# Order of TensorE's work within a chunk: expert sums ahead of the next half's mixer slices

## The reference

```python
x = x + y @ w_out                    # y: pooling, window attention, short convolution, differential attention
x = x + peer_ffn(rms_norm(x, norm2_g), w_query, sub_keys, peer_u, peer_v)
...
h = jnp.einsum('thkd,td->thk', peer_u[ib], xb)       # 8 heads x 16 experts of each token, out of 16384
a = (gb * jax.nn.gelu(h, approximate=False)).astype(xb.dtype)
out = jnp.einsum('thk,thkd->td', a, peer_v[ib])
```

## Time and profile before

| | |
|---|---|
| median of 3 runs | 2962.0 us (2955.64 to 2963.01) |
| the profiled execution's own time | 2951.57 us |
| its span | 2949.8 us |
| PE busy | 2097.7 us, 71% |
| DVE busy | 2065.5 us, 70% |
| ACT busy | 1041.2 us, 35% |
| gathers | 1024, 1073.81 MB, 87.8% of 16 DMA engines' span |
| mean granted clock of TensorE | 0.842 |

### The profile page before, as it was taken

One profiled execution on the slowest core, in us unless ns is written; L12 is line 12 of the kernel. 1 busy time (PEld: TensorE's weight loads), 2 busy tenths in 40 slices (PEclk: granted clock), 3 DMA queues, 4 the chain that ended last, 5 costly groups with the idle time before them and its releaser, 6 DMA issues.

```text
span 2949.8 us, 37238 instructions
## 1 busy us (share of the span) xinstructions
PE 2097.7 (71%) x12696; PEld 1036.4 (35%) x12696; DVE 2065.5 (70%) x5215; ACT 1041.2 (35%) x3347; POOL 1194.0 (40%) x1028
## 2 busy tenths in 40 slices
PE   8888787777777876586775877667776665656565
PEld 7554454344443432243342533234343111111111
DVE  2466678977567687867567678976766766777665
ACT  2322345633233455423223345632223222222222
POOL 0034334443344334444343434543444444444443
PEclk9988999888888987888887988889898678677768
DMA  6189999999999999999999999999999999999998
GB/s 233 36 345 418 419 419 419 395 420 419 419 419 419 420 414 414 417 384 420 420 420 420 416 386 420 421 386 419 420 420 421 421 421 421 418 418 420 419 415 341
DMA packets 174350, 1173.26 MB, mean 398 GB/s; under 512 B 19280, under 2 KB 19408, under 8 KB 43088
## 3 DMA queue, kind: packets, MB, share of 16 engines
q0 software_dynamic: 147456, 1073.81, 87.8%
q1 hardware_dynamic: 26704, 97.07, 8.4%
HBM read 1168.71 MB, written 2.10 MB: 397 GB/s over the span
## 4 chain that ended last, share of the span: by engine, by line
DMA 48%; PE 22%; DVE 18%; ACT 5%; issue 5%; POOL 1%; SPq 0%; DVEq 0%; POOLq 0%; ACTq 0%
DMA gather<-experts,idx 48%; PE ysum L686 12%; DVE gather L1259 9%; PE bank L466 6%; ACT amp L915 2%; POOL gather L421 1%; ACT diag L923 1%; PE ysum L474 1%; PE bank L661 1%; ACT gel L908 1%; DVE x L1235 1%; PE bank L515 1%; DVE shared L1045 0%; DVE scratch L1206 0%; DVE scratch L1210 0%
## 5 line engine op out<-in xcount | busy, mean ns | idle before, releaser
L421 POOL DMA_INDIRECT gather<-experts,idx x1024 | 1193.8, 1166 | 1733.8 <-PE ysum L686 1411.5
L686 PE MATMUL ysum<-gather,diag 64*64 64x512 f32 x8192 | 1263.2, 769 | 728.3 <-ACT diag L923 696.7
L1259 DVE CUSTOM_DVE_ANT_0 gather<-gather,xc 128x1024 f32<-128x1024 f32 x1024 | 1229.8, 1224 | 682.8 <-DMA gather<-experts,idx 680.0
L686 PEld LDWEIGHTS ysum<-gather,diag 64*64 64x64 f32 x8192 | 365.7, 172 | 1526.9 <-ACT diag L923 906.8
L908 ACT ACTIVATE gel<-hdot 128x4 f32<-128x4 f32 x255 | 52.4, 205 | 1679.4 <-DVE hdot L1259 1679.4
L466 PE MATMUL bank<-xnT,w 128*128 128x256 f32 (+1 forms) x2048 | 467.1, 384 | 5.9 <-DVE xnT L975 5.9
L466 PEld LDWEIGHTS bank<-xnT,w 128*128 128x128 f32 x2048 | 380.0, 194 | 100.6 <-issue 42.8
L923 ACT ACTIVATE diag<-cc,amp 128x64 f32<-128x64 f32 x1020 | 267.9, 333 | 0.0
L915 ACT ACTIVATE amp<-gel,gate 128x1 f32<-128x1 f32 x1020 | 216.8, 283 | 8.3
L908 ACT ACT_TABLE_LOAD x105 | 134.7, 1283 | 1.8
L661 PEld LDWEIGHTS bank<-w,yT 128*128 128x128 f32 x768 | 87.3, 192 | 17.8 <-issue 17.8
(11 more groups left out here) (126 smaller groups left out, 1490.2 us busy)
## 6 DMA issues: line engine op xcount, KB each, us to landing
w<-weights SPq DMA_DIRECT2D x164, 512.0 KB, 7.9
gather<-experts,idx POOLq DMA_INDIRECT x1024, 15.1
gather<-weights SPq DMA_DIRECT2D x4, 1024.0 KB, 5.6
y_out<-x SPq DMA_DIRECT2D x4, 512.0 KB, 7.8
x<-x_in SPq DMA_DIRECT2D x2, 512.0 KB, 5.3
g2b<-g_rows SPq DMA_DIRECT2D x2, 512.0 KB, 11.7
x<-x_in SPq DMA_DIRECT2D x1, 1024.0 KB, 12.4
cc<-consts_in SPq DMA_DIRECT2D x1, 920.5 KB, 6.4
```

Of the source, the lines that this page charges most:

```text
L421: pool.indirect_dma_start(gather[:, n % SLOTS, :], None, uv_d[m // 2], bass.IndirectOffsetOnAxis(ap=idx[:, g % 2, k:k + 1], axis=0)).then_ ...
L686: mm = nc.tensor.matmul(ysum[outs, q * 512:(q + 1) * 512], diag[toks, n % NDIAG, :], gather[toks, n % SLOTS, DM + hf * 512:DM + (hf + 1) * ...
L1259: e = V.tensor_tensor_reduce(out=gather[:, n % SLOTS, 0:DM], in0=gather[:, n % SLOTS, 0:DM], in1=xc[:, :], scale=1.0, scalar=0.0, op0=ALU. ...
```

## The change

PE's call of `interleave` loses its argument, and so takes the order that ACT and DVE have: first Y(c), then S(c).

```diff
             for m in range(NBLK):
-                interleave(m, lambda n: mixer_pe(pe, n), peer_pe(pe, m), first, slices_first=True)
+                interleave(m, lambda n: mixer_pe(pe, n), peer_pe(pe, m), first)
```

## The result

The changed kernel takes 3364.91 us in the median of three runs (3355.66 to 3365.22), against 2962.0 us before: ratio 1.1358, 95% interval 1.1343 to 1.1373, 403 us slower. The forecast was 3360.

What follows compares the result with a forecast made beforehand. The prediction took DMA to set the pace everywhere, 10.0 to 12.5 us a chunk. Its terms 35 + 86 + 63 + 120 + 100 + 24 - 30 = 398 us gave 3350, or 3360 as median, range 3210 to 3510.

Steps and rivals of the forecast that it cites:

- Y(c): PE's expert sums of chunk c, which wait for ACT's diagonals; forecast at 6.0 us, ends 3.7 and 6.7.
- S(c): PE's slice of chunk c; forecast 1.0 or 1.4 us in attention, 3.84 in output blocks, 5.1 with a projection.
- Y of 6.0 us: PE's expert sums in each chained chunk, behind 7 us or more of idle time, take 6.0 us, not 6.67.
- cushion: Ten gather slots let DMA work on through a delay: about 10 us forgiven once in each section, -30 us.
- Attention: Chunks where DVE's biases wait for PE's scores: +86, +35 and +63 us in sections 1, 2 and 3.
- Output blocks: Chunks where DVE's addition waits for PE's block: turn 16.6 us against DMA's 11.25, +120 us over three sections.
- Plain projections: Chunks where ACT, not DVE, closes the chain: one block costs nothing, two take 14.1 against 12.5, 15 times: +24 us.
- Transitions: Chunks with transposes, last value block, first biases and norms of y: together +100 us.
- ACT's path in sections 1 and 3: Eight attention slices with a projection: ACT's copy, table loads and exponential make the longer chain, 16.5 us a turn.
- No change: Rival: DMA hides the new order, with DVE's gather waits and ten slots as slack; 2962 us, chance 0.03.
- Faster: Rival: gather slots come free earlier and the DMA dips fill, 25 us less, 2937 us; chance 0.02.
- Y at 3.7: Rival, slower by half: PE's clock stays up, expert sums take 3.7 to 4.6 us, time 3150 to 3235; chance 0.10.

Runs made afterwards that it cites:

- the last run: Kernel before, with PE's expert sums first only in the three chunks with the norms of y: 2951.45 us, ratio 0.9989 to the kernel before.
- narrow sums: Changed kernel, all four products of every second gather run over 128 of 512 columns: 3232.52 us, ratio 1.0937 to the kernel before.
- wide ones: Changed kernel, the four products of every fourth gather issued twice: 3446.74 us, ratio 1.1667 to the kernel before.

## Why the prediction was right, step by step

*DMA sets the pace before, 10.0 to 12.5 us a chunk.* Right as far as it was tried: with the sums longer by a quarter the kernel before stayed where it was. No run changed the gathers themselves.

*The chain closes where DVE's slice needs PE's of the same chunk.* Right, and shown from both sides: taking ACT's and DVE's slices a chunk later takes the whole loss away, DVE's alone 271 us of it, and the order matters little in chunks without the link (+19 us).

*Turns.* Output block: forecast 16.6, 16.8 in the turn shown and 16.3 as the mean of the seven turns of section 2 (113.8 us from its first L1166 to its last). In the turn shown Y took 6.61 us and not 6.0, with which the parts of the forecast give 17.2, so the closeness of 16.6 and 16.8 is in part luck. Attention of section 3: forecast 16.1, 17.0 in the turn shown (Y 6.45 us in it), an item over all 512 keys, where biases and scores are longer than the 384-column rows that I used.

*Y of 6.0 us.* 5.86. Choosing the level of the rows with gaps above 4 us over the 6.67 of a single one was right. By the stricter reading of the clock rule in the Trainium skill (TensorE: Matmul & The Clock Gate, "What's actually happening") the sum would have been 60 us higher; the 88 rows of Y behind gaps above 4 us, 5.86 us in the mean, speak against that size.

*Sizes of the parts.* A part that is changed alone has the forecast's whole cushion of 30 to itself. Attention: forecast 184, so 154 with the cushion off, and +194 when changed alone: too small. Output blocks: 120, so 90, and +100 alone. Plain projections: 24, so nothing, and +19 alone; the turn of two blocks was also added up wrongly (its rows give 14.3 and not 14.1, some 4 us in all). Transitions: 100, so 70, and +41 alone: too large. There the forecast counted every chunk at full excess and took nothing off for the wait that the sums escape at the norms of y, which is worth 3 to 4 us by the last run. Why the remainder was too large is open. Within the changed kernel the stretches from the first bias to the last grew by 169 us, against the 184. By section the forecast has 166, 101 and 131 when its terms and 10 us of cushion each are sorted (plain ones 18, 3 and 3; transitions 35, 30 and 35, a split made after the result); measured 173, 94 and 142. The errors of the terms cancel to some 10 us, and that is luck: the total agrees better than its terms. The cushion itself was measured by no run.

*ACT's path in sections 1 and 3.* The direction is supported by the run with DVE a chunk later (section 2 and all output blocks back, the attention of sections 1 and 3 not); its share is not settled, as said above.

*What would show it.* DMA at 6 to 8 and some 300 GB/s in the stretches: 292 GB/s in the window of section 3. In section 2 the slices with attention kept a 9, at 355 to 368 GB/s. Waits at L1045 and L1166: 468 us in place of 29. DVE's waits for gathers were to fall to some 300 and fell to 507: those of the last section (177 us before) and of the plain projections stayed, and I had not set them aside.

*Rivals.* No change needed DVE's slice not to wait; it waits. Faster: the fixed part of the turn (4.7 + 1.5 + Y) is above DMA's 10 us. Y at 3.7 did not come: PE's gaps in the turns shown are 6 to 8 us. The advice to work on the most-contended engine (the Trainium skill, Perfetto Trace Analysis, "Identifying Performance Opportunities") would have left this edit at nothing; read in that way it does not hold here: PE was busy 71% of the span, DMA's row stood at 9, and the edit, which touches PE's order alone, cost 13.6%.

## What to carry to other kernels

When work of several engines is interleaved by hand, look where the same slice stands on each of them: the producer's part should lie ahead of the long step that its user does first. Before an order is changed on an engine that has time to spare, follow one turn through the in-order queues of all engines and add it up; if the turn is closed and longer than the pace of the bound engine, slack in busy time does not help. A buffer of ten slots forgives a delay once (some 10 us by the estimate of the forecast, not measured), not 5 us in every chunk.

## What the hardware showed that was not expected

Leaving out three of four products in every second gather made the sums no shorter: 20 records of a chunk last as long as 32.

```profile
2255.67 6.21 PE L687 MATMUL ysum<-gather,diag 64*64 64x512 f32 x20 [6.89 <-ACT diag L924]
```

In the changed kernel 32 records behind the same gap of 6.89 us last 6.39 us (at 2203.12 above). Products of 64 by 64 in different quarters of the array overlap, so their number is not their cost.

The granted clock moves against a change of PE's work: 0.757 with narrow sums, 0.814 in the changed kernel, 0.850 with wide ones. Leaving out 3/8 of the columns shortened Y by 26%, and adding a quarter lengthened it by 14%. In these runs a change of cost scaled from the columns alone came out too large, in both directions.
